# Feed-forward first products: one matmul of 512 columns for both operand halves, added on the way out

## What is computed

```python
def swiglu(x, w1, w3, w2):
    return (jax.nn.silu(x @ w1) * (x @ w3)) @ w2
# x: 256 x 1024, w1 and w3: 1024 x 2816, w2: 2816 x 1024; twice, once for each layer
```

## Time and profile before

| | us |
|---|---|
| median of 3 runs | 1844.67 (1843.20 to 1845.51) |
| the profiled execution, device time | 1842.88 |
| its span in the trace | 1841.2 |
| TensorE busy | 1765.5 (96%) |
| weight loads (PEld) busy | 1588.9 (86%) |
| VectorE busy | 1241.8 (67%) |
| ScalarE busy | 904.7 (49%) |

### The profile page before, as it was taken

How to read it: one execution, slowest core, us unless ns; L and a number is a source line. 1 busy time by engine, 2 the same in 40 slices (tenths; PEclk the granted TensorE clock), 3 DMA queues, 4 the chain that set the end, 5 groups by cost and what they waited for, 6 DMA issues and landing times.

```text
span 1841.2 us, 32433 instructions
## 1 busy us (share of the span) xinstructions
PE 1765.5 (96%) x11628; PEld 1588.9 (86%) x11628; DVE 1241.8 (67%) x2320; ACT 904.7 (49%) x1590; POOL 209.8 (11%) x148
## 2 busy tenths in 40 slices
PE   8969999999999999898989999999999999999997
PEld 7747999878979997797779999999998998888886
DVE  4367766686667666866646884777886656666666
ACT  4633443356644443646335545777774444333333
POOL 1021000011110000021112788000000000000000
PEclk9979999999999999999989999999999999999999
DMA  6453656745436667344214455444444555555553
GB/s 207 158 191 126 248 198 217 280 149 176 166 118 220 230 233 244 127 159 144 77 64 151 161 180 176 149 142 143 141 138 168 186 183 183 192 183 189 187 186 133
DMA packets 86359, 317.60 MB, mean 172 GB/s; under 512 B 9632, under 2 KB 9904, under 8 KB 85488
## 3 DMA queue, kind: packets, MB, share of 16 engines
q1 hardware_dynamic: 77328, 279.48, 44.6%
q10 hardware_dynamic: 7200, 25.45, 3.9%
q0 software_dynamic: 1728, 11.25, 1.6%
HBM read 315.08 MB, written 1.05 MB: 172 GB/s over the span
## 4 chain that ended last, share of the span: by engine, by line
PE 67%; DVE 5%; ACT 3%; issue 2%; DMA 1%; POOL 0%; ACTq 0%; DVEq 0%; POOLq 0%
PE bank L244 20%; PE bank L246 20%; PE bank L245 20%; PE bank L2199 3%; DVE wl L199 1%; DMA ada<-in_w_ada 1%; ACT wh L192 1%; PE bank L489 1%; PE bank L524 0%; PE bank L559 0%; DVE ada L325 0%; PE bank L2043 0%; PE bank L523 0%; DVE xl L368 0%; PE bank L490 0%
## 5 line engine op out<-in xcount | busy, mean ns | idle before, releaser
L192 ACT ACTIVATE wh<-ring 128x1024 fp32r<-128x1024 f32 x529 | 558.9, 1059 | 760.1 <-PE bank L246 717.1
L199 DVE TENSOR_TENSOR wl<-ring,wh 128x1024 fp32r<-128x1024 f32 x479 | 585.9, 1226 | 448.3 <-ACT wh L192 448.1
L244 PE MATMUL bank<-xh,wh 128*128 128x256 f32 x2072 | 596.8, 288 | 6.8 <-DVE xl L368 6.6
L246 PE MATMUL bank<-xh,wl 128*128 128x256 f32 x2072 | 588.7, 284 | 0.0
L245 PE MATMUL bank<-xl,wh 128*128 128x256 f32 x2072 | 588.4, 284 | 0.0
L244 PEld LDWEIGHTS bank<-xh,wh 128*128 128x128 f32 x2072 | 399.7, 193 | 10.4 <-issue 7.7
L245 PEld LDWEIGHTS bank<-xl,wh 128*128 128x128 f32 x2072 | 399.5, 193 | 1.1
L246 PEld LDWEIGHTS bank<-xh,wl 128*128 128x128 f32 x2072 | 399.0, 193 | 0.0
L244 PE MATMUL bank<-wh,wa_high 128*128 128x512 f32 x512 | 202.5, 396 | 2.1 <-DVE weighted L2218 1.4
L246 PE MATMUL bank<-wh,wa_low 128*128 128x512 f32 x512 | 202.1, 395 | 0.0
L245 PE MATMUL bank<-wl,wa_high 128*128 128x512 f32 x512 | 202.0, 395 | 0.0
(11 more groups left out here) (431 smaller groups left out, 2237.8 us busy)
## 6 DMA issues: line engine op xcount, KB each, us to landing
ring<-in_stream SPq DMA_DIRECT2D x529, 512.0 KB, 3.3
ada<-in_w_ada ACTq DMA_DIRECT2D x48, 512.0 KB, 4.4
rows<-in_rows POOLq DMA_DIRECT2D x1, 2560.0 KB, 13.5
rows<-in_rows POOLq DMA_DIRECT2D x2, 1024.0 KB, 5.2
con<-in_early POOLq DMA_DIRECT2D x1, 1374.0 KB, 17.5
x_feature_major<-in_x_fm SPq DMA_DIRECT2D x4, 256.0 KB, 5.2
x<-in_x_tm POOLq DMA_DIRECT2D x1, 1024.0 KB, 5.0
weighted<-in_subkeys POOLq DMA_DIRECT2D x1, 1024.0 KB, 5.3
```

Of the source, the lines that this page charges most:

```text
L192: C.activation(wh[q % AHEAD][:, :], ring[slot][:, :], ACT.Copy).then_inc(s_high, 1)
L199: low.tensor_tensor(wl[q % AHEAD][:, :], ring[slot][:, :], wh[q % AHEAD][:, :], ALU.subtract).then_inc(s_low, 1)
L244: T.matmul(o, left[0], right[0], start=start, stop=False, skip_group_check=True)
L246: return T.matmul(o, left[1], right[0], start=False, stop=stop, skip_group_check=True)
```

## The change

`xh` and `xl` become two views of one tile `xs` of 128 x 8 x 2 x 256, so that for each k the high and the low half lie side by side, 512 columns in a row. In the first products the three matmuls of a step k become two: w_high times all 512 columns of `xs[:, k]`, into a whole bank (left half: w_high x_high; right half: w_high x_low), and w_low times x_high, 256 columns, onto the left half. The two halves of the bank are added when they are read: ScalarE copies the right half into SBUF, VectorE adds the left half to it. The Silu is then taken from SBUF, and the final multiply reads SBUF alone. The semaphores count 5 steps of VectorE and 3 of ScalarE for a tile.

```diff
-    xh = sb(base, "xh", [P, KD, S], F32R)
-    xl = sb(base, "xl", [P, KD, S], F32R)
+    xs = sb(base, "xs", [P, KD, 2, S], F32R)
+    xh, xl = xs[:, :, 0, :], xs[:, :, 1, :]
...
+        def wide(g, k, h, l):
+
+            ks = slice(k * P, (k + 1) * P)
+            T.matmul(g[:, :], h[:, ks], xs[:, k, :, :].rearrange("p a t -> p (a t)"), start=k == 0, stop=False,
+                     skip_group_check=True)
+            return T.matmul(g[:, 0:S], l[:, ks], xh[:, k, :], start=False, stop=k == KD - 1, skip_group_check=True)
+
...
-                    last = mm3(bank[3 * piece][:, 0:S], (h[:, k * P:(k + 1) * P], l[:, k * P:(k + 1) * P]),
-                               (xh[:, k, :], xl[:, k, :]), k == 0, k == KD - 1)
+                    last = wide(bank[3 * piece], k, h, l)
...
-                        T.wait_ge(s_gate, 3 * n3 + 3 * (u - 3) + 1 if i is not None else 3 * (u - 3) + 1)
+                        T.wait_ge(s_gate, n15 + 5 * (u - 3) + 2)
...
-                        last = mm3(g[:, 0:S], (h[:, k * P:(k + 1) * P], l[:, k * P:(k + 1) * P]),
-                                   (xh[:, k, :], xl[:, k, :]), k == 0, k == KD - 1)
+                        last = wide(g, k, h, l)
...
-                        C.wait_ge(s_gate, 3 * n3 + 3 * (u - 3) + 1)
-                    C.activation(sg[u % 3][:, :], ga[:, 0:S], ACT.Silu).then_inc(s_silu, 1)
-            V.wait_ge(s_used, s + (q + 2))
-            V.wait_ge(s_silu, n3 + (u + 1))
-            V.tensor_tensor(hf[u % 3][:, :], sg[u % 3][:, :], gb[:, 0:S], ALU.mult).then_inc(s_gate, 1)
-            V.wait_ge(s_gate, 3 * n3 + (3 * u + 1))
+                        C.wait_ge(s_gate, n15 + 5 * (u - 3) + 3)
+                    C.activation(sg[u % 3][:, :], ga[:, S:2 * S], ACT.Copy).then_inc(s_silu, 1)
+                    V.wait_ge(s_silu, n9 + (3 * u + 1))
+                    V.tensor_tensor(sg[u % 3][:, :], ga[:, 0:S], sg[u % 3][:, :], ALU.add).then_inc(s_gate, 1)
+            C.wait_ge(s_gate, n15 + (5 * u + 1))
+            C.activation(sg[u % 3][:, :], sg[u % 3][:, :], ACT.Silu).then_inc(s_silu, 1)
+            C.wait_ge(s_used, s + (q + 2))
+            if i is not None or u >= 3:
+                C.wait_ge(s_gate, n15 + 5 * (u - 3) + 5)
+            C.activation(hf[u % 3][:, :], gb[:, S:2 * S], ACT.Copy).then_inc(s_silu, 1)
+            V.wait_ge(s_silu, n9 + (3 * u + 3))
+            V.tensor_tensor(hf[u % 3][:, :], gb[:, 0:S], hf[u % 3][:, :], ALU.add).then_inc(s_gate, 1)
+            V.wait_ge(s_gate, n15 + (5 * u + 2))
+            V.tensor_tensor(hf[u % 3][:, :], sg[u % 3][:, :], hf[u % 3][:, :], ALU.mult).then_inc(s_gate, 1)
+            V.wait_ge(s_gate, n15 + (5 * u + 3))
...
-        gated_in = lambda k: pe.wait((s_gate, 3 * max(k + 1, KF - 2)))
+        gated_in = lambda k: pe.wait((s_gate, 5 * max(k + 1, KF - 2)))
```

More of the change, by code:

```diff
@@ L1085, in tile @@
             n3 = 0 if i is None else i * 3
+            n9 = 0 if i is None else i * 9
+            n15 = 0 if i is None else i * 15
             s = 0 if i is None else i * BODY
@@ L1119, in tile @@
             V.tensor_copy(hrow, hf[u % 3][:, :]).then_inc(s_gate, 1)
-            V.wait_ge(s_gate, 3 * n3 + (3 * u + 2))
+            V.wait_ge(s_gate, n15 + (5 * u + 4))
             V.tensor_tensor(lrow, hf[u % 3][:, :], hrow, ALU.subtract).then_inc(s_gate, 1)
@@ L1702, in opened @@
         pe.wait(zr)
-        T.matmul(bank[4][:, :], zrow[:, :], xh[0:1, 0:2, :].rearrange("p a t -> p (a t)"), start=True, stop=False,
+        T.matmul(bank[4][:, :], zrow[:, :], xs[0:1, 0, :, :].rearrange("p a t -> p (a t)"), start=True, stop=False,
                  skip_group_check=True)
```

## The result

The changed kernel takes 1838.38 us (median of 12 runs, 1833.71 to 1841.19), the kernel before 1844.24 (12 runs, 1841.06 to 1845.51): ratio 0.9970, 95% interval 0.9961 to 0.9978. It is faster by 5.9 us, between 4.1 and 7.2. The forecast was 1832.1, a gain of 12.6. So the direction and the range (1829 to 1842) hold, and more than half of the gain is missing.

The account below looks back on a forecast made before the run. The kernel was taken as bound by TensorE, in the feed-forwards by the pitch of its matmuls. Saving 14.1 - 1.0 - 0.45 = 12.6 us took 1844.67 to 1832.1; range 1829 to 1842.

Parts of the forecast that it names:

- So I take 227: First products: a wide 512-column matmul costs 227 ns, as in a row with x stationary and weights moving; 235 the bound.
- So I take 113: First products: a 256-column matmul behind a wide one costs 113 ns instead of 120; 120 the bound.
- The term of 14.1 us: First products: 704 steps at 340 ns instead of 360 save 14.1 us.
- first rival: First products: wide or short matmul dearer, 347 to 355 ns per step, time 1836.3 to 1841.6; chance 0.19.
- Rows 4 has the tiles of the change: Argument for 227 ns: that profile excerpt shows 512-column matmuls on the same two tiles, with stationary and moving roles exchanged.
- the place in the trace that mixes widths: Expert stage: a 512-column matmul takes 0.23 us, the first 256-column one behind it 0.11, the next 0.12.
- The reading behind 113: TensorE: weight loads set the short pitch; a long matmul lets them get ahead some 7 ns, used by the first short one.
- No gain at all: First products: a 512-column matmul takes 240 ns, the step stays 360, time about 1845; chance 0.09.
- The way out: Draining PSUM: VectorE gains 0.81 us per tile, 5.54 against TensorE's 5.44 in tiles 0 to 3; ScalarE's 3.2 is hidden.
- The first tiles and the end: TensorE stalls: 0.5 us per layer in the first tiles, 1.0 in all, and 0.45 at the end of layer 1.
- the chain of w_ada: End of layer 1: VectorE's reductions and w_ada DMAs start later by 0.44 us, priced as 0.45 us of TensorE stall.
- The ring: Weight loads landing in 6.0 us instead of 3.7 cost 20 us over 18 tiles, 1852; chance 0.12, including VectorE's waits.

Follow-up runs that it names:

- the 32 bytes of padding: 32 bytes put behind xs (behind xl in the kernel before), moving ring, wh and wl: kernel before 1832.14 us, ratio 0.9937; changed kernel 1831.79 us, ratio 0.9936.
- drain-only kernel: Changed kernel with its wide matmul issued as two of 256 columns, keeping the new ScalarE and VectorE work: 1841.76 against 1842.72 us, ratio 0.9994.
- the kernel in groups of eight: Changed kernel with all eight wide matmuls of a piece ahead of its eight short ones (tile 0 in twos): 1835.94 us in one execution.
- the changed kernel with three pads: Changed kernel with three pads of 32 bytes, putting x at 32 within 64 bytes, w and h at 0: 1830.83 us, ratio 0.9935.

## Why the prediction was right or wrong

**The step that failed: the matmuls.** "So I take 227" and "So I take 113" took the price of a wide matmul from a uniform row and that of a short one from the one place behind a wide one, and added them. Each was read rightly: the wide one is 226.7 ns in a row of its kind even with the tiles of the change, and 113 does occur behind a wide one. Together they are not what the row of the change does: 236 + 117 = 353 ns or 232 + 115 = 347, not 340. The term of 14.1 us is 4.7 in one pattern and 9.2 in the other. The text named this as its first rival (347 to 355 ns, 1836.3 to 1841.6) and gave it a chance of 0.19, and the median of 1838.38 lies between its two ends. "Rows 4 has the tiles of the change" was the argument against it, and the place in the trace that mixes widths was read for one short pitch only. It has no wide matmul behind the short ones, so it can't show what the next wide one costs.

**The reading behind 113.** I explained it by the weight loads getting ahead during a long matmul. For the short ones it fits: behind eight wide ones they took 113, 119 and then 120. It says nothing of the wide ones, which I priced at 227 in any row, and there the 7 ns went: behind short ones they took 228 to 241. The faster pattern, 347, is what the two uniform rows add up to (226.7 + 120), so nothing of the 7 ns is left in it, and the slower one costs 6.6 more. That weight loads are the reason isn't shown, and no other reason is.

**No gain at all** fell: a step is not 360 ns. The Trainium skill, TensorE: Matmul & The Clock Gate, section Back-to-back issue gap, gives 262 cycles for 256 columns and 518 for 512, from which I had estimated 6 cycles or 2.5 ns for a fused pair. The runs show 6.7 to 13 per step, so that estimate is too low here, and mine of 20 was too high. With the 32 bytes of padding it is near: there a step went from 355 to 353 ns.

**The way out** was right, instruction by instruction. VectorE's tile 1 was forecast at 5.54 us and took 5.52 (timeline of VectorE, in the changed kernel):

```profile
192.22 1.22 DVE L199 TENSOR_TENSOR wl<-ring,wh 128x1024 fp32r<-128x1024 f32 x1
193.36 0.42 DVE L1120 TENSOR_TENSOR silu<-bank,silu 128x256 f32<-128x256 f32 x1
193.69 1.22 DVE L199 TENSOR_TENSOR wl<-ring,wh 128x1024 fp32r<-128x1024 f32 x1
194.82 0.42 DVE L1128 TENSOR_TENSOR h_full<-bank,h_full 128x256 f32<-128x256 f32 x1
195.28 0.43 DVE L1130 TENSOR_TENSOR h_full<-silu,h_full 128x256 f32<-128x256 f32 x1
...
197.74 1.22 DVE L199 TENSOR_TENSOR wl<-ring,wh 128x1024 fp32r<-128x1024 f32 x1
```

The table load stands ahead of the first Silu as forecast, 1.28 us, and VectorE then waited 0.53 us for the Copy of hf, not 0.9. The Copies take 366 ns (376 in the earlier trace rows). The drain-only kernel shows the sum of it, a ratio of 0.9994.

**The first tiles and the end.** I priced 1.0 us for VectorE in tiles 0 to 3 and 0.45 for the chain of w_ada. Both came out smaller: TensorE's tile is 5.65 or 5.55 us, not 5.44, so VectorE's 5.52 is hidden, as the text says for a slower TensorE, and only tile 2 of each layer is longer, by 0.15 us. Behind the chain of w_ada TensorE waited 0.44 us, and 0.36 before. These two terms were too dear by about 1.1 us, which hid an eighth of the 9.4 us by which the first was too high in the slower pattern. That was luck.

**The ring** was named as the way to slower, with the w_ada and rows loads as its cause. In the profiled execution it did occur, at 7.2 us to land. It cost 1.8 us and not 20, since only the two loads behind the 1 MB one were late, and not every one in 18 tiles. The trace of before had the same place at 5.6 us; with a median of 3.7 in the earlier trace rows I didn't look for the longest.

**What stays open**: why wide matmuls behind short ones cost more than in a row of their kind, what picks one of the two patterns, and why the offset of 32 bytes helps rows of 256 columns and harms those of 512.

## What to carry to other kernels

A pitch from a row of equal matmuls doesn't add up with that of another row: where a change mixes widths, its price is that of the mixed row. Here the two uniform pitches would make 346.7 ns, and the row took 347 to 353; with the pad they would make 351.5, and it took 347 to 353 again. What one matmul saves by its neighbour, look for in the next one. When the columns stay the same, only a part of what the matmuls take beyond them can be won, here 7 to 13 ns of 360; a change of 32 bytes in where a tile stands was worth more than that and is the cheaper thing to try. And for a ring of loads, look at its longest landing and at what was issued just ahead of it, and not only at the median.

## What was not expected of the hardware

- A row of alternating 512 and 256 columns settles in one of two repeating patterns, 353.3 or 347 ns per pair, within one program and at the same granted clock of 1.00; it was seen to change only where the row had been delayed, once by 10 to 20 ns.
- Behind 256-column matmuls those of 512 take 228 to 236 ns up to the fifth, and 226.7 from the sixth on; behind 512-column ones the first of 256 takes 113, the second 119, and the others 120 (the kernel in groups of eight).
- The offset of the tiles, varied by 32 bytes: with x and w both at 0 of 64, 119.9 ns for 256 columns and 227 to 228 for 512; with w at 32, 118.2 and 233 to 234. For h stationary it is 234.3 (h at 32, w at 0) and 232.6 (both at 0). For the kernel before, one pad is a ratio of 0.9937.
- TensorE starts layer 1 at the lower clock level (1.2 GHz) in both kernels, after an idle time of 2.46 us. The windows of TensorE behind it, in the kernel before and in the changed one, and two rows of the latter:

```profile
546.60:549.00 2.40, 2.35 (x12) 0.56 0.08 32
```

```profile
547.40:549.50 2.10, 2.10 (x7) 0.50 0.09 35
```

```profile
547.40 0.77 PE L1074 MATMUL bank<-xs,wh 128*128 128x512 f32 x1 [2.46 <-DVE xs L368]
...
548.17 0.63 PE L1074 MATMUL bank<-xs,wh 128*128 128x512 f32 x1
```

  A granted clock of 0.50 with 7 matmuls in 2.1 us; a wide one lasts 0.63 us in the place of 0.40, until 550.1. The first tile takes 7.01 us in the place of the 5.63 of layer 0, so it costs some 1.4 us, and 1.5 before (7.32 and 5.83). The idle time alone doesn't decide it. The second profile of the changed kernel had the lower level in layer 0 too, behind the same 2.06 us of idle time as the first, which had 1.00 there; the changed kernel with three pads kept 1.00 in layer 1 behind 2.46 us; and in the kernel before with one pad the clock fell in layer 0 only 1.4 us after TensorE had resumed. This is one source of the differences between executions.
